# Linear-attention levels made among the projections, rotary turns dealt over half slots, coarse blocks inside the head norm

## The reference

```python
rel = cum[:, :, :, None, :] - cum[:, :, None, :, :]
decay = jnp.exp(jnp.where(mask[:, :, None], rel, -jnp.inf))
attn = jnp.einsum('bhid,bhjd,bhijd->bhij', qc, kc, decay)
o = o_inter + jnp.einsum('bhij,bhje->bhie', attn, vc)
...
od = diff_attend(qd, jnp.concatenate([kd_c, kd], axis=2), jnp.concatenate([vd_c, vd], axis=2), lam)
mix = jnp.concatenate([gla_merge(og, r, gla_norm_g[l]), diff_merge(od, diff_norm_g[l], lam_init)], axis=-1) @ w_out[l]
```

## Time and profile before

| | us |
|---|---|
| median of 3 runs | 2065.51 (2064.54 to 2067.44) |
| profiled execution | 2066.24 |
| its span | 2064.4 |
| PE busy | 1959.6 (95% of the span) |
| DVE, ACT, POOL busy | 921.6, 745.1, 702.8 |
| the chain that ended last, PE's share | 86% |

### The profile page before, as it was taken

How to read it: one execution, slowest core, us unless ns; L and a number is a source line. 1 busy time by engine, 2 the same in 40 slices (tenths; PEclk the granted TensorE clock), 3 DMA queues, 4 the chain that set the end, 5 groups by cost and what they waited for, 6 DMA issues and landing times.

```text
span 2064.4 us, 26644 instructions
## 1 busy us (share of the span) xinstructions
PE 1959.6 (95%) x10526; PEld 1542.8 (75%) x10530; DVE 921.6 (45%) x1346; ACT 745.1 (36%) x1236; POOL 702.8 (34%) x295
## 2 busy tenths in 40 slices
PE   7999988689999999999999999899999999999998
PEld 4787856567888888788888867556866768888886
DVE  2742586844444420544443235676875532232102
ACT  4533365433222211423232144546256432222222
POOL 1421110423444444344444433220421433444442
PEclk9999999799999999999999999899999999999999
DMA  7851110023444542344345422210310222232231
GB/s 307 303 205 42 42 62 1 22 62 112 151 144 139 176 153 94 110 145 150 133 171 184 163 78 82 62 44 10 101 52 32 82 83 91 92 102 91 94 100 61
DMA packets 60129, 223.23 MB, mean 108 GB/s; under 512 B 6800, under 2 KB 7056, under 8 KB 58384
## 3 DMA queue, kind: packets, MB, share of 16 engines
q1 hardware_dynamic: 59472, 219.70, 31.5%
q10 hardware_dynamic: 576, 2.43, 0.3%
HBM read 220.00 MB, written 2.10 MB: 108 GB/s over the span
## 4 chain that ended last, share of the span: by engine, by line
PE 86%; DVE 7%; ACT 3%; issue 2%; DMA 1%; SPq 0%; DVEq 0%; ACTq 0%
PE ps L445 75%; PE ps L1056 1%; DMA early_raw<-early 1%; DMA mod_w<-mod_w 1%; PE ps L591 1%; DVE neg_max L1201 1%; PE ps L1075 1%; PE ps L2269 1%; PE ps L2440 1%; PE ps L2461 0%; DVE ps L697 0%; PE ps L2291 0%; PE ps L2431 0%; PE ps L978 0%; PE ps L2449 0%
## 5 line engine op out<-in xcount | busy, mean ns | idle before, releaser
L1858 POOL TENSOR_TENSOR w_lo<-raw,w_hi 128x1024 fp32r<-128x1024 f32 x276 | 667.3, 2418 | 1290.5 <-ACT w_hi L458 691.3
L445 PE MATMUL ps<-hh,w_hi 128*128 128x512 f32 (+1 forms) x1512 | 604.5, 400 | 20.4 <-DVE hl L683 10.6
L445 PE MATMUL ps<-hl,w_hi 128*128 128x512 f32 (+1 forms) x1512 | 595.2, 394 | 0.0
L445 PE MATMUL ps<-hh,w_lo 128*128 128x512 f32 (+1 forms) x1512 | 595.2, 394 | 0.0
L445 PEld LDWEIGHTS ps<-hh,w_hi 128*128 128x128 f32 (+1 forms) x1512 | 287.3, 190 | 93.4 <-issue 29.3
L445 PEld LDWEIGHTS ps<-hh,w_lo 128*128 128x128 f32 (+1 forms) x1512 | 287.0, 190 | 62.1
L445 PEld LDWEIGHTS ps<-hl,w_hi 128*128 128x128 f32 (+1 forms) x1512 | 287.5, 190 | 58.4
L1831 ACT ACTIVATE w_hi<-raw 128x1024 fp32r<-128x1024 f32 x126 | 133.7, 1061 | 477.2 <-PE ps L445 477.2
L511 DVE SCALAR_TENSOR_TENSOR mod_raw<-mod_raw,cond_ada 128x1024 f32<-128x1024 f32 x72 | 116.2, 1616 | 247.9 <-DMA mod_raw<-late 247.9
L445 PE MATMUL ps<-act_hi,w_hi 128*128 (+1 forms) x528 | 208.8, 396 | 0.0
L445 PE MATMUL ps<-act_lo,w_hi 128*128 (+1 forms) x528 | 208.8, 396 | 0.0
(11 more groups left out here) (441 smaller groups left out, 2293.5 us busy)
## 6 DMA issues: line engine op xcount, KB each, us to landing
raw<-stream SPq DMA_DIRECT2D x284, 512.0 KB, 3.5
mod_raw<-late SPq DMA_DIRECT2D x72, 512.0 KB, 4.4
early_raw<-early SPq DMA_DIRECT2D x32, 512.0 KB, 5.9
mod_w<-mod_w SPq DMA_DIRECT2D x8, 1024.0 KB, 20.3
xT<-xT SPq DMA_DIRECT2D x2, 1024.0 KB, 6.2
xT<-xT ACTq DMA_DIRECT2D x2, 1024.0 KB, 6.9
out<-fin SPq DMA_DIRECT2D x8, 256.0 KB, 2.2
cT<-cT SPq DMA_DIRECT2D x1, 1024.0 KB, 21.7
```

The source lines that it names most:

```text
L445: mm = pe.matmul(out, w, r, start=first and i == 0, stop=last and i == 2)
L1858: pool.tensor_tensor(lo[:, :], raw[n % RING][:, :], hi[:, :].bitcast(F32), ALU.subtract)\
```

## The change

The chunks of the projections come in another order: gate inputs and linear keys before the softmax keys, linear values before softmax values. The context always uses bank 2, sums of squares bank 3. Two gates are made at once in slots 11 and 13, on banks 4 to 7. Turns 0 to 3 (queries) stand in slots 14 (two of them, one after each half), 15 and 16, and turns 4 to 7 (keys) in slots 21 to 24. The rotation works in place: its sine part goes back to the bank, and the rest to the tensor itself.

Level 0's products stand in slot 15, the five fine levels' in slots 17 to 21, all in banks 6 and 7; the spans, exponentials and products with queries and keys of all seven levels run in slots 15 to 22. The level buffers take the place in memory that `xT` takes again later, so `xT` is loaded again only after the last coarse products.

The coarse products are cut in halves of two banks: three halves are made before the last pair's transposes, the fourth after the last pair's values and ahead of the last head's squares. ACT and DVE copy two halves each. The sums of the head norm go to bank 6. What is left at the end is states, then `within`. The exponentials and products of the queries with running sums (`qe`) and the copies of `diag` are made before or among the mixed chunks.

Names in the rows of order: a `ps` is a bank, `lq`/`lk` and `level_q`/`level_k` are the level buffers.

```diff
-    gate = [sb(f"gate{i}", [P, NALL]) for i in range(4)]
-    top[0] -= 4 * NALL * 4
+    level_q = [sb(f"level_q{i}", [P, 2 * N]) for i in range(2)]
+    level_k = [sb(f"level_k{i}", [P, 2 * N]) for i in range(2)]
+    top[0] -= 4 * 2 * N * 4
     xT = sb("xT", [P, KD, N])
...
     chunks_a = ([("gq", i, GQ + i * P, P, False) for i in range(2)] + [("dq", h, DQ + h * P, P, False) for h in range(HEADS)]
-                + [("gr", h, GR + h * P, P, False) for h in range(HEADS)] + [("dk", h, DK + h * P, P, True) for h in range(HEADS)]
-                + [("gd", 0, GD, 32, True)] + [("dv", h, DVC + h * P, P, True) for h in range(HEADS)]
-                + [("gk", i, GK + i * P, P, True) for i in range(2)] + [("gv", h, GV + h * P, P, True) for h in range(HEADS)])
+                + [("gr", h, GR + h * P, P, False) for h in range(HEADS)] + [("gd", 0, GD, 32, True)]
+                + [("gk", i, GK + i * P, P, True) for i in range(2)] + [("dk", h, DK + h * P, P, True) for h in range(HEADS)]
+                + [("gv", h, GV + h * P, P, True) for h in range(HEADS)] + [("dv", h, DVC + h * P, P, True) for h in range(HEADS)])
-    AT_NC, AT_SUMS, AT_TURNS, AT_GATES = 4, 8, 17, 16
+    AT_NC, FIRST_BOTH, AT_QUERY_SUMS, AT_KEY_SUMS, AT_SPREADS, AT_LEVELS = 4, 10, 8, 15, 22, 16
+    GATES_AT = {11: (0, 1), 13: (2, 3)}
+    TURNS_EARLY = {14: 0}
+    TURNS_AT = {14: 1, 15: 2, 16: 3, 21: 4, 22: 5, 23: 6, 24: 7}
+    SUMS_AT = {AT_QUERY_SUMS + h: h for h in range(HEADS)} | {AT_KEY_SUMS + h: HEADS + h for h in range(HEADS)}
...
-            for key, b, rh, rl, tokens, key_norm in ((("x", i), i % 2, hh, hl, N, "nx"), (("c", i), 2 + i % 2, ch, cl, NCTX, "nc"))[:1 + both]:
+            for key, b, rh, rl, tokens, key_norm in ((("x", i), i % 2, hh, hl, N, "nx"), (("c", i), 2, ch, cl, NCTX, "nc"))[:1 + both]:
...
-                    if i > AT_TURNS and (i - AT_TURNS) % 2 == 0:
-                        context_spread(pe, (i - AT_TURNS) // 2 - 1)
+                    if i >= AT_SPREADS:
+                        context_spread(pe, i - AT_SPREADS)
+                    if i in TURNS_EARLY:
+                        diff_turn(pe, TURNS_EARLY[i])
+                    if i == AT_LEVELS - 1:
+                        level_products(pe, 0)
+                    if AT_LEVELS < i <= AT_LEVELS + FINE:
+                        level_products(pe, level_order[i - AT_LEVELS - 1])
-            if AT_GATES <= i < AT_GATES + len(directions):
-                gates_tensor(pe, i - AT_GATES)
+            for z in GATES_AT.get(i, ()):
+                gates_tensor(pe, z)
...
-            if AT_SUMS <= i < AT_SUMS + 2 * HEADS:
-                diff_sums(pe, i - AT_SUMS)
-            if i >= AT_TURNS:
-                diff_turn(pe, i - AT_TURNS)
+            if i in SUMS_AT:
+                diff_sums(pe, SUMS_AT[i])
+            if i in TURNS_AT:
+                diff_turn(pe, TURNS_AT[i])
...
             ins = act.activation(x_to, ps[0:width, b, 0:N], func, scale=scale).then_inc(bank_empty(b), 1)
+            if i == AT_LEVELS:
+                level_decay(act, 0)
             if both:
...
-                diff_square(act, i - AT_SUMS + 1)
-            for key, at in (("nq", AT_SUMS + HEADS), ("nk", AT_SUMS + 2 * HEADS)):
+            if i + 1 in SUMS_AT:
+                level_decay(act, i - AT_LEVELS + 1)
+            for key, at in (("nq", AT_QUERY_SUMS + HEADS), ("nk", AT_KEY_SUMS + HEADS)):
...
+            if i and chunks_a[i - 1][0] in ("dv", "gv"):
+                values_vector(dve, *chunks_a[i - 1][:2])
+            if i == AT_LEVELS - 1:
+                level_masked(dve, 0)
+            if AT_LEVELS < i <= AT_LEVELS + FINE:
+                level_masked(dve, level_order[i - AT_LEVELS - 1])
+            if i >= AT_SPREADS:
+                context_keys(dve, i - AT_SPREADS)
+            if i in TURNS_EARLY:
+                diff_rotate(dve, TURNS_EARLY[i])
+            for z in GATES_AT.get(i - 2, ()):
+                gates_vector(dve, z)
+            if i in (AT_LEVELS - 2, AT_LEVELS - 1):
+                for j in (2 * (i - AT_LEVELS + 2), 2 * (i - AT_LEVELS + 2) + 1):
+                    running_sums(dve, j)
+            if i == AT_LEVELS - 1:
+                settle(dve, "cum_ready")
+                level_spans(dve, 0)
+            if AT_LEVELS <= i < AT_LEVELS + len(level_order):
+                level_queries(dve, i - AT_LEVELS)
+            if i == AT_LEVELS:
+                diff_rotate(dve, TURNS_AT[i])
+            if AT_LEVELS <= i < AT_LEVELS + len(level_order) - 1:
+                level_spans(dve, i - AT_LEVELS + 1)
...
+        mark("rope_step", dve.tensor_tensor(ps[:, b, :], ps[:, b, :], ca("sin"), ALU.mult))
+        mark("rope_step", dve.scalar_tensor_tensor(out=x, in0=x, scalar=gains, in1=ca("cos"), op0=ALU.mult, op1=ALU.mult))
         settle(dve, "rope_step")
-        dve.tensor_tensor(t1[1][:, 0:N], t1[1][:, 0:N], t1[0][:, 0:N], ALU.add).then_inc(bank_empty(b), 1)
+        dve.tensor_tensor(x, x, ps[:, b, :], ALU.add).then_inc(bank_empty(b), 1)
         read(dve, ("rot_" + key, h))
         b = full(dve, ("rs_" + key, h))
-        dve.tensor_tensor(x, t1[1][:, 0:N], ps[:, b, :], ALU.mult).then_inc(S("diff_rotated"), 1)
+        dve.tensor_tensor(x, x, ps[:, b, :], ALU.mult).then_inc(S("diff_rotated"), 1)
     def context_spread(pe, h):
...
+            if u == len(pairs) - 1:
+                for b in range(6):
+                    bank_freed[b] = (S("diff_exp"), max(part for part in range(2 * len(pairs)) if part % 3 == b // 2) + 1)
+                level_coarse(pe, 1, 0)
+                level_coarse(pe, 1, 1)
+                level_coarse(pe, 2, 0)
             turn(u, "tA", range(4), "probT_a")
             if u:
                 mix_values(u - 1)
             turn(u, "tB", range(4, NTA), "probT_b")
-        for b in range(6):
-            bank_freed[b] = (S("diff_exp"), max(part for part in range(2 * len(pairs)) if part % 3 == b // 2) + 1)
...
+        for h in range(HEADS - 1):
+            head_squares(h)
         mix_values(len(pairs) - 1)
-        for h in range(1, HEADS):
-            head_squares(h)
+        level_coarse(pe, 2, 1)
+        head_squares(HEADS - 1)
...
-            if u == 2:
-                act.wait_ge(S("cum_ready"), len(directions))
-                act.wait_ge(S("cumc_ready"), len(directions))
-                for i in range(2):
-                    act.dma_start(xT[:, 4 * i:4 * i + 4, :], A["xT"][:, 4 * i:4 * i + 4, :]).then_inc(S("x_again"), 16)
         act.activation(root_first[:, :], c("eps"), ACT.Sqrt)
+        blocks_scalar(act, 1, 0)
         later_tiles(last)
         outputs(last - 1)
         outputs(last)
+        blocks_scalar(act, 2, 1)
+        for i in range(2):
+            act.dma_start(xT[:, 4 * i:4 * i + 4, :], A["xT"][:, 4 * i:4 * i + 4, :]).then_inc(S("x_again"), 16)
...
+        blocks_vector(dve, 2, 0)
+        full(dve, ("pv", len(pairs) - 1))
+        blocks_vector(dve, 1, 1)
...
+    def level_buffers(li):
+        n = level_order.index(li)
+        return level_q[n % 2], level_k[n % 2] if LEVELS[li - 1] > 1 else gkx[:, :, :].rearrange("p c n -> p (c n)")
+    def level_products(pe, li):
+        q, k = level_buffers(li) if li else (gqx[:, :, :].rearrange("p c n -> p (c n)"), gkx[:, :, :].rearrange("p c n -> p (c n)"))
+        if li:
+            n = level_order.index(li)
+            pe.wait_ge(S("lq_ready"), n + 1)
+            pe.wait_ge(S("lk_ready"), level_counts(n)[1])
+        else:
+            read(pe, ("x", chunk_of[("gk", 1)]))
+        if li == 0 or li > COARSE:
             for half in range(2):
-                claim(pe, fine_bank[li] + half, ("level", li, half))
+                claim(pe, 6 + half, ("level", li, half))
...
+    COARSE_BANKS = {(1, 0): 4, (1, 1): 0, (2, 0): 2, (2, 1): 4}
+    def level_coarse(pe, li, part):
+        q, k = level_buffers(li)
+        n = level_order.index(li)
+        pe.wait_ge(S("lq_ready"), n + 1)
+        pe.wait_ge(S("lk_ready"), level_counts(n)[1])
+        for half in range(2):
+            b = COARSE_BANKS[(li, part)] + half
+            claim(pe, b, ("level", li, 2 * part + half))
+            rows = slice(64 * half, 64 * half + 64)
+                at = (j % 2) * N + (2 * part + j // 2) * P
+                mm = pe.matmul(ps[:, b, j * P:(j + 1) * P], k[rows, at:at + P], q[rows, at:at + P], start=True, stop=True)
+            mm.then_inc(bank_full(b), 1)
...
+    def level_decay(act, n):
+        li = level_order[n]
+        sums, _ = level_counts(n)
+        q, k = level_buffers(li)
+        if LEVELS[li - 1] > 1:
+            act.wait_ge(S("level_sums"), sums - 2)
+            act.activation(k[:, :], k[:, :], ACT.Exp, scale=GATE_SCALE).then_inc(S("lk_decay"), 1)
+        act.wait_ge(S("level_sums"), sums)
+        act.activation(q[:, :], q[:, :], ACT.Exp, scale=GATE_SCALE).then_inc(S("lq_decay"), 1)
+    def level_queries(dve, n):
+        q, _ = level_buffers(level_order[n])
+        dve.wait_ge(S("lq_decay"), n + 1)
```

(69 more changed lines are left out.)

229 lines of the change are left out of this document (77 added, 152 removed).

## The result

| | before | after |
|---|---|---|
| median | 2065.61 us (4 runs) | 2040.36 us (2035.55 to 2044.05, 4 runs) |
| ratio | | 0.9875, interval 0.9860 to 0.9889 |
| profiled execution (span) | 2066.24 (2064.4) | 2041.45 (2039.6) |

The change makes the kernel 1.2% faster, 25.2 us in the medians; 30.0 were forecast (2035.5, range 2029.5 to 2047). The forecast holds, 4.9 us low. The busy time by stage of the kernel after answers to the earlier trace rows: the projections from their slot 8 to the last turn in two pieces, then the last values of the softmax attention, the mixed chunks but the first, the states and `within`.

What follows compares the result with a forecast made beforehand. PE alone was taken to bound the projections, a DVE, ACT and POOL chain the levels, DVE the head norm's end. Terms -35.7 - 3.0 - 1.3 + 10.0 = -30.0 gave 2036.2 us profiled, 2035.5 median, range 2029.5 to 2047.

Steps and rivals of the forecast that it cites:

- Term 1: End of the linear attention: all level products leave, only two sets for the states stay, 39.9 - 4.2, so -35.7 us.
- Term 3: First 24 matmuls of `within`: PE no longer idle ahead, so 3 x 1.00 instead of 4.31 us, -1.3.
- Term 2: Head norm and keys: first mixed chunk ends 1.9 us earlier, wait of 1.07 for keys goes, -3.0 in all.
- Term 4: Projections: PE receives six levels at 1.22 us, 7.3, plus 2.7 of "issue" gaps, +10.0 us.
- third rival: Projections: PE waits for levels and its clock falls, up to 8.5 us per slot, +85 in ten, 2120; chance 0.04.
- Stalls behind the port: Projections, slots 15 to 22: DVE slowed beside POOL, five fine levels each 2.2 us late, +11, 2046.5; chance 0.17.
- `xT` late: Mixed chunks: load lands in 18 us rather than 6.9, PE waits some 6.5 us for a bank, 2042; chance 0.08.
- The clock falling behind waits: Projections: waits for levels lower PE's clock, up to 8.5 us more per slot, 2120 if in all ten; chance 0.04.
- the work not hidden: Projections: PE waits 6.1 us in each of five fine levels, 30 us eat the gain, about 2065; chance 0.03.

Runs made afterwards that it cites:

- level-0 edit: Kernel before, with level 0's products in the head norm on banks 2 and 3 instead of 0 and 1: 2062.27 us, ratio 0.9978.
- reordered kernel: Changed kernel with two coarse halves before the last pair, two behind the last head's squares, no ACT block copies ahead of the root: 2037.91 us, ratio 0.9859.
- kernel with the root first: Changed kernel, ACT's root before eight block copies and xT loads, last coarse half on banks 2 and 3, first key transposes later: 2039.90 us, ratio 0.9869.
- second profile: Changed kernel unedited, run and profiled again in the second job: profiled execution 2036.11 us, median 2038.45 us, ratio 0.9876.

## Why the prediction was right

**Bounds.** That PE alone sets the projections, a chain through DVE the levels, and DVE's bank the head norm is borne out three times: by PE's single wait of 0.4 us, by 3.77 us in place of 39.89, and by the kernel before with level 0 in other banks.

**Term 1** (-35.7): measured -36.1. The two sets for the states took 3.77 us, 0.5 less than two of the earlier trace rows, and no bank or `qe` is waited for. **Term 3** (-1.3): -1.4.

**Term 2** (-3.0) is the step that failed: measured +3.3 in the head norm and -1.2 in the chunks behind it, +2.1 in all. The reading behind it was right, as the level-0 edit shows, and so was the wait of 1.07: from the root (L1455, L1565) to the end of the first mixed chunk it is 8.70 us instead of 12.76, 4.1 less, where the term had 4.3 (2.4 late, 1.9 early). What failed lies ahead of the root. It comes 15.10 us behind the last probabilities instead of 7.76, 7.3 later, where the term had 2.4. Two costs set against it were too small. I had put three coarse halves "at nothing beyond the 2.4" into PE's wait before the last pair; they take 3.86 us and the wait held 1.3, so the transposes come 2.5 later than they could. I had named 4.2 as their bound and then taken the near end without laying the two lengths side by side, though both could be read. And I let PE's other work run beside ACT's at full clock. At the low clock the last values take 2.77 us instead of 1.46, and the coarse half behind them 1.66 instead of 1.28, all of it ahead of the last head's squares; behind the root the spreads take 3.90 instead of two times 1.06. The low clock is there again in the reordered kernel (3.02 us for 16, at 0.50). What brings it down no run shows: the kernel before made the same squares and values at 1.00. ACT's copies ahead of the root cost 1.0 by the kernel with the root first, and not 2.4. So 2.5 for the early halves, 1.3 for the values, 1.7 for the late half and these 1.0 make 6.5 of the 7.3.

**Term 4** (+10.0): +7.9 without a fall of the clock, +12.6 in the first profile. The chains of the kernel before and of the second profile take the 7.9 apart by line. The six levels are 7.3, as in the sum. The 744 matmuls of the chunks took 133.9 us instead of 132.7: a context half behind other work takes 3.02 and not 2.80, and there are more of these. The sums of squares took 0.2 more, turns and gates together 0.8 less. So the part that was mis-sized is the 2.7 of gaps: PE has no gap there at all. (By the Trainium skill's "Runtime: NRT & Kernel Launch", section "Instruction fetch mechanics", fetching is mostly hidden; here the trace agrees.) The 4.7 us between the two profiles are the falls of the clock, which I hadn't considered at all: the third rival looked for them behind waits, and they came without any. The prediction's 6 to 7 us of DVE's work per slot were low, too: it worked 82.71 us in the eleven slots from 14 on, some 7.5 in each.

**The sum.** The undisturbed execution took 2036.11 us, and the sum had said 2036.2. That is luck in part: the four terms measured are -27.5, and 2.6 us came from the stretch up to slot 8 and the softmax attention, which the sum left alone. The clock was higher there than in the profile of before (0.89 against 0.83 in the first 30 us, 0.98 against 0.93 in the attention); that this is the cause isn't shown. The three medians lie 1.4 to 4.2 us above 2036.2, for the most part by the falls if the three profiles stand for the rest.

**The rivals.** Stalls behind the port: the contention is there (2.67 and 2.88 against 0.68), the stalls are not; 5.8 to 7.0 us more on DVE in four slots running made PE wait 2.5 in all. `xT` late: it is issued 15 us later than I had it, and its first addition at 370.87 still held nobody up, since PE has no wait on a bank there. The clock falling behind waits, and the work not hidden: not seen in the changed kernel.

## What to carry to other kernels

Work moved under a bound engine costs its length, and a little where it splits a stream (0.2 us for a context half here); the slack of the other engines swallowed even a fourfold slowdown beside POOL. Gaps read from rows between waits were not there in the dense stream. Where short matmuls are put into a wait, lay their summed length against that wait's own row before calling it free. And a wait called "issue" before an engine writes a bank deserves a look at who emptied the bank last: one bank number gave back 5 us.

## What the hardware showed unexpectedly

PE's granted clock fell while PE was busy without a gap. Busy time of the kernel after, first profile, behind the two gates of slot 11 (columns as in the earlier trace rows):

```profile
116.00:120.00 4.00, 4.00 (x16) 2.71 (x15) 2.59 (x3) 3.82 (x8) 2.86 (x1) 0.82 1.00 347
120.00:124.00 4.00, 4.00 (x11) 3.13 (x12) 3.00 (x5) 3.96 (x6) 0.36 (x1) 0.50 0.92 332
124.00:128.00 4.00, 4.00 (x16) 3.23 (x15) 3.14 (x5) 2.68 (x3) 0.00 (x0) 0.82 0.99 380
```

0.50 is the lower of the two levels, 1.2 GHz. The four chunk parts there took 19.20 us, and 16.66 in the second profile. What PE did before the fall was a chunk of 32 columns (98 to 107 us), a full chunk, four matmuls of 32 rows and sums of two columns; the kernel before, in which the gates stand apart, has 1.00 throughout in two profiles. But the falls come in some executions and not in others of the same program. Of the eight profiles with the gates in pairs six have one or two falls; of the three with the gates apart one has a single fall (56.19 us) and two have none. That speaks for the gates in pairs, but with so few profiles it shows nothing, and ACT's work on the gates beside them was tested by no run. The cause stays open. The Trainium skill, page "TensorE: Matmul & The Clock Gate", section "HAM oscillation — how this bites in real kernels", ties such falls to idle gaps of PE; in these rows PE has none, as far as a profile with modelled ends of matmuls can tell, so here the measurement says otherwise.
